# First opening's loads split by use, half 0's forward transform in PSUM banks 4 to 7, three offset adds on VectorE

## What is computed

```python
mod = silu(c) @ w_ada[l] + b_ada[l]                 # the "ada" pieces
u, gate = adaln_modulate(h, mod)                    # the opening
p = split_proj(u @ w_in[l])

def hyena_filter_spectrum(n, ...):                  # in the opening too
    h = sin(fr * (h @ w + b))                       # three times: the "net" steps
    h = (h @ w4).reshape(n, ORDER, 2, W) * exp(-t * deltas)   # the "tap" steps
    return rfft(full)                               # the "blk" steps

def hyena_mix(xv, gate, conv_w, spec, bias):
    x1, x2, v = split(depthwise_conv(xv, conv_w), 3)
    z = x1 * long_conv(v, 0)                        # order 0
    z = x2 * long_conv(z, 1)                        # order 1
    return z * silu(gate)

h = layer_norm(ALPHA * h + gate * out) * ln_g + ln_b    # gained, then the offset
```

## Time and profile before

| | us |
|---|---|
| median of 3 runs (all: 2884.63, 2884.56, 2879.94) | 2884.56 |
| the profiled execution | 2881.1 |
| its span | 2879.3 |
| TensorE busy in it | 2697.6 (94%) |
| VectorE busy | 1601.5 (56%) |
| ACT busy | 1013.9 (35%) |
| GpSimd busy | 590.3 (21%) |

### The profile page before, as it was taken

How to read it: one execution, slowest core, us unless ns; L and a number is a source line. 1 busy time by engine, 2 the same in 40 slices (tenths; PEclk the granted TensorE clock), 3 DMA queues, 4 the chain that set the end, 5 groups by cost and what they waited for, 6 DMA issues and landing times.

```text
span 2879.3 us, 50275 instructions
## 1 busy us (share of the span) xinstructions
PE 2697.6 (94%) x21222; PEld 2152.7 (75%) x21222; DVE 1601.5 (56%) x2789; ACT 1013.9 (35%) x1642; POOL 590.3 (21%) x243
## 2 busy tenths in 40 slices
PE   7899998999999999999999999888899999999997
PEld 1388777887888888887787438677778787887775
DVE  4745777427564443436747654667537754453756
ACT  0335444222222343224432234454333334423533
POOL 0022000120113211321024312100140132232036
PEclk8999999999999999999999999999999999999998
DMA  7321000332222112220134551100143231231034
GB/s 248 137 73 47 16 20 16 110 110 88 75 87 88 66 52 98 86 81 30 39 113 152 196 183 53 37 14 14 54 160 103 100 117 55 97 116 59 25 115 168
DMA packets 94237, 251.71 MB, mean 87 GB/s; under 512 B 10466, under 2 KB 28132, under 8 KB 93632
## 3 DMA queue, kind: packets, MB, share of 16 engines
q1 hardware_dynamic: 83322, 220.84, 22.7%
q10 hardware_dynamic: 10694, 27.67, 2.6%
HBM read 207.05 MB, written 34.08 MB: 84 GB/s over the span
## 4 chain that ended last, share of the span: by engine, by line
PE 74%; DVE 16%; ACT 4%; issue 3%; DMA 2%; ACTq 1%; POOL 0%; SPq 0%; DVEq 0%
PE ps L912 17%; PE ps L913 17%; PE ps L914 17%; PE ps L920 4%; PE ps L1494 4%; PE ps L1051 2%; PE ps L1521 2%; PE ps L929 2%; DVE t_gcv L2175 1%; PE ps L1504 1%; PE ps L1006 1%; PE ps L1518 1%; PE ps L1097 1%; PE ps L1366 1%; DVE t_grp L2509 1%
## 5 line engine op out<-in xcount | busy, mean ns | idle before, releaser
L873 POOL TENSOR_TENSOR t_wlo<-t_raw,t_whi 128x1024 fp32r<-128x1024 f32 x230 | 568.5, 2473 | 2258.2 <-ACT t_whi L1615 2258.2
L912 PE MATMUL ps<-t_u_hi,t_whi 128*128 128x512 f32 (+1 forms) x2368 | 859.0, 363 | 17.5 <-issue 3.7
L913 PE MATMUL ps<-t_u_lo,t_whi 128*128 128x512 f32 (+1 forms) x2368 | 835.1, 353 | 0.0
L914 PE MATMUL ps<-t_u_hi,t_wlo 128*128 128x512 f32 (+1 forms) x2368 | 830.8, 351 | 0.0
L1615 ACT ACTIVATE t_whi<-t_raw 128x1024 fp32r<-128x1024 f32 x248 | 262.1, 1057 | 843.0 <-PE ps L914 765.8
L912 PEld LDWEIGHTS ps<-t_u_hi,t_whi 128*128 128x128 f32 x2368 | 450.0, 190 | 91.7 <-issue 24.1
L914 PEld LDWEIGHTS ps<-t_u_hi,t_wlo 128*128 128x128 f32 x2368 | 448.3, 189 | 63.6
L913 PEld LDWEIGHTS ps<-t_u_lo,t_whi 128*128 128x128 f32 x2368 | 450.3, 190 | 56.7 <-issue 1.7
L1686 ACT ACTIVATE t_grp<-ps 128x512 f32<-128x512 f32 (+2 forms) x236 | 104.1, 466 | 228.8 <-PE ps L929 107.7
L2778 DVE TENSOR_REDUCE t_amx<-ps 128x1 f32<-128x768 f32 (+1 forms) x120 | 101.5, 846 | 148.8 <-PE ps L1494 148.1
L2167 DVE TENSOR_TENSOR t_yv<-t_oT,t_sil 128x768 f32<-128x768 f32 (+1 forms) x32 | 67.4, 2107 | 174.6 <-ACT t_sil L1686 174.6
(11 more groups left out here) (282 smaller groups left out, 3870.3 us busy)
## 6 DMA issues: line engine op xcount, KB each, us to landing
t_raw<-in_w_in SPq DMA_DIRECT2D x184, 512.0 KB, 3.5
t_raw<-in_w_ada SPq DMA_DIRECT2D x48, 512.0 KB, 4.4
t_raw<-in_w_br SPq DMA_DIRECT2D x32, 512.0 KB, 3.6
t_raw<-in_w_out SPq DMA_DIRECT2D x32, 512.0 KB, 3.7
t_sg<-gate_logits SPq DMA_DIRECT2D x28, 384.0 KB, 4.5
hs<-t_hstage ACTq DMA_DIRECT2D x20, 512.0 KB, 3.7
t_hring<-hs SPq DMA_DIRECT2D x20, 512.0 KB, 5.4
t_prob<-t_pT ACTq DMA_DIRECT2D x56, 128.0 KB, 2.1
```

The lines of the kernel that those rows point to most:

```text
L873: pool.tensor_tensor(wlo[:, c % CONV, :], raw[:, s % RAW, :], whi[:, c % CONV, :].bitcast(f32), ALU.subtract).then_inc(sems["w_ready"], 1)
L912: pe.matmul(o, lh, rh, start=first, stop=False)
L913: pe.matmul(o, lh, rl, start=False, stop=False)
L914: return pe.matmul(o, ll, rh, start=False, stop=last)
```

## The change

- Step "w4" of layer 0's opening goes ahead of ada group 1.
- ACT's loads of layer 0: w4 and bias behind net 0; the four context decays behind net 1, on ld_par; the constants behind net 2, ahead of the latent decays, the residual tiles and the masks; the masks count on ld_h. The waits' numbers follow.
- In both layers and both orders, the forward transform of half 0 of the latents goes to banks 6, 7 (odd) and 4, 5 (even); the transposes of tiles 2 and 3 go to slots 0 and 1, each to the slot of the projection that it reads. TensorE's wait for `hinv` goes from ahead of the forward transform to ahead of the inverse; ACT's copy goes from behind tile 3's conv step to behind the second copy into z, one projection earlier.
- In layer 1, VectorE makes the offset adds of tiles 0 to 2 right behind `gained`, instead of GpSimd.

```diff
         yield "turn", 0, 0
+        yield "w4", 0, 0
         for q in range(4):
             yield "ada", 1, q
-        yield "w4", 0, 0
...
+        def forward_at(st, m):
+
+            return 0 if st or m else 4
...
-                if s + 1 == len(STREAM) or STREAM[s + 1][0] != l:
-                    for i in range(NT if l == 0 else LT - 1):
-                        pool.wait_ge(sems["wo_g"], (NT if l else 0) + i + 1)
+                if l == 0 and STREAM[s + 1][0] != l:
+                    for i in range(NT):
+                        pool.wait_ge(sems["wo_g"], i + 1)
...
                         if st and a == 0:
-                            pe.wait_ge(sems["ld_c"], 112)
+                            pe.wait_ge(sems["ld_c"], 96)
...
                     for lo, name, reader in ((2, "f_fo", "hy_oc"), (0, "f_ev", "hy_ps")):
-                        claim(lo, lo + 1)
+                        at = forward_at(0, m) + lo
+                        claim(at, at + 1)
...
                     if o == 0:
-                        freed["hy_oc"] = freed.get("hy_oc", 0) + 1
-                        pe.wait_ge(sems["hy_oc"], freed["hy_oc"])
+                        pe.wait_ge(sems["ld_ftab"], 16 * (23 if l else 14))
+                        freed["hy_oc"] = turned = freed.get("hy_oc", 0) + 1
...
-                            to_tok(o, m, freed["cv_done"] + m - 3, m)
+                            to_tok(o, m, freed["cv_done"] + m - 3, (nslot[0] + m) % 2)
...
+                            if o == 0:
+                                pe.wait_ge(sems["hy_oc"], turned)
                             ln.take("hy_y")
...
+                        if a == 1 and l == 0:
+                            for dst, src in context_decays():
+                                act.dma_start(dst, src).then_inc(sems["ld_par"], 16)
+                        if a == 2 and l == 0:
                             act.dma_start(cst[:, 1:8, :], A["cst"][:, 1:8, :]).then_inc(sems["ld_c"], 16)
-                        if a == 2 and l == 0:
...
-                            act.dma_start(mask_f[:, :], A["masks"]).then_inc(sems["ld_c"], 16)
+                            act.dma_start(mask_f[:, :], A["masks"]).then_inc(sems["ld_h"], 16)
...
-                    if o == 0:
-                        act.wait_ge(sems["ld_ftab"], 16 * (23 if l else 14))
-                        ln.done(run(hinv[:, :, :, :], y[:, 1, 0:2 * LAT].rearrange("p (e s r) -> p e r s", e=2, r=CLASS),
-                                    ACT.Copy), "hy_oc")
+                        if j == 2 and o == 0:
+                            act.wait_ge(sems["ld_ftab"], 16 * (23 if l else 14))
+                            ln.done(run(hinv[:, :, :, :],
+                                        y[:, 1, 0:2 * LAT].rearrange("p (e s r) -> p e r s", e=2, r=CLASS), ACT.Copy),
+                                    "hy_oc")
...
-            def gained(i):
+            def gained(l, i):
 
                 ln.take("wo_x")
                 x = acc_t[:, i, :]
                 ln.done(tt(x, x, lng[:, 0, :], ALU.mult), "wo_g")
+                if l and i < LT - 1:
+                    ln.own("wo_g")
+                    ln.done(tt(x, x, lng[:, 1, :], ALU.add), "wo_out")
...
+                    if l == 0 and x == 0 and t == 0:
+                        dve.wait_ge(sems["ld_par"], 112)
                     if l == 0 and x == 2 and t == 0:
-                        dve.wait_ge(sems["ld_h"], 16 * (NT + 16))
+                        dve.wait_ge(sems["ld_h"], 16 * (NT + 17))
```

More of the change, by code:

```diff
@@ L544, in latent_decays, with context_decays @@
                     yield dec[32 * k:32 * k + 32, r, :], A["dec"][r:P:CLASS, k, :]
+        def context_decays():
+            for r in range(CT):
+                for half in range(2):
+                    yield dec[64 * half:64 * half + 64, LT + r, :], A["dec"][r:P:2, LT + half, :]
         def filter_inputs(l):
@@ L551, in filter_inputs @@
                 yield from latent_decays()
-            for r in range(CT):
-                for half in range(2):
-                    yield dec[64 * half:64 * half + 64, LT + r, :], A["dec"][r:P:2, LT + half, :]
+                yield from context_decays()
         def residual(l, i):
@@ L1362, in forward @@
                     for lo, name, reader in ((2, "f_fo", "hy_oc"), (0, "f_ev", "hy_ps")):
-                        claim(lo, lo + 1)
+                        at = forward_at(0, m) + lo
+                        claim(at, at + 1)
                         for r in range(lo, lo + 2):
                             for e in range(2):
-                                last = pe.matmul(ps[:, r, e * 256:e * 256 + 256], htab[:, r, e, :],
+                                last = pe.matmul(ps[:, at + r - lo, e * 256:e * 256 + 256], htab[:, r, e, :],
                                                  z[:, r, m * 256:m * 256 + 256], start=True, stop=True)
                         ln.done(last, name)
-                        lend(reader, lo, lo + 1)
+                        lend(reader, at, at + 1)
                 def inverse(m, i):
@@ L1991, in hyena @@
                             odd[0] += 1
-                            ln.done(run(h_odd[:, :, :], ps[:, 2:4, :], ACT.Copy), "hy_oc")
+                            x = forward_at(st, m) + 2
+                            ln.done(run(h_odd[:, :, :], ps[:, x:x + 2, :], ACT.Copy), "hy_oc")
                         elif st:
@@ L2292, in open_layer @@
                     if kind == "masks":
-                        dve.wait_ge(sems["ld_c"], 112)
+                        dve.wait_ge(sems["ld_c"], 96)
+                        dve.wait_ge(sems["ld_h"], 16 * (NT + 17))
                         full = mask_f[:, :].rearrange("p (a b c) -> p a b c", a=2, b=LEVELS)
@@ L2325, in open_layer @@
                     if kind == "gain":
-                        gained(a)
+                        gained(l - 1, a)
                     if kind == "stat":
@@ L2631, in apart @@
                         dve.wait_ge(sems["hy_iv"], i - 1)
-                    tt(two[:, 0, :, :], ps[:, 0:2, :], h_odd[:, :, :], ALU.add)
-                    ln.step(tt(two[:, 1, :, :], ps[:, 0:2, :], h_odd[:, :, :], ALU.subtract), "hy_ps")
+                    tt(two[:, 0, :, :], ps[:, x:x + 2, :], h_odd[:, :, :], ALU.add)
+                    ln.step(tt(two[:, 1, :, :], ps[:, x:x + 2, :], h_odd[:, :, :], ALU.subtract), "hy_ps")
                     dve.wait_ge(sems["hy_tr"], turned)
@@ L2853, in project_out @@
                     if kind == "gain":
-                        gained(a)
+                        gained(l, a)
             for l in range(DEPTH):
```

20 lines of the change are left out of this document (10 added, 10 removed).

## The result

| | before | after |
|---|---|---|
| median, us (runs) | 2882.25 (2879.29 to 2884.63, 4) | 2858.81 (2855.68 to 2868.26, 4) |
| profiled execution, us (span) | 2881.1 (2879.3) | 2861.72 (2859.9) |

The ratio is 0.9926 (95%: 0.9902 to 0.995): 23.4 us faster between the medians, 19.4 between the two profiled spans. The forecast was 2851, with 31.5 us of gain; the measured time is inside its range, and it is also the figure of rival A, 2859.

What follows compares the result with a forecast made beforehand. TensorE, busy 94% of the span, was taken as the bound. Opening 12.5 plus Hyena 20.0 minus tail 1.0 gave 31.5 us, so 2849.6 from the profiled 2881.1, predicted as 2851 us; range 2837 to 2866.

Steps and rivals of the forecast that it cites:

- rival A: Opening: loads move no sooner, masks still land near 67 us, opening gains 5 to 8 us; 2859 us, chance 0.12.
- Group 1's piece, 5.3 us: Opening, TensorE: without 1 MB of loads beside its w_ada piece, group 1 ends near 26.0 instead of 31.3 us.
- w4's sum moved, first tap 5.0 us earlier: Opening: VectorE sums w4 before group 1's row, so TensorE's first tap starts at 36.9 instead of 41.91 us.
- Masks' wait on TensorE, 5.7 and 1.45 us: First context transform: the 5.71 us wait on the masks' counter goes, and its 8 matmuls run 1.45 us faster.
- Masks' landing at 60.7: Opening: masks land at 60.7 instead of 67.0 us; VectorE's first latent tap wants them at 59.7.
- The slow clock of 40 to 50 us, 3.3 us: Opening, two taps and the w_ada group between: a shorter TensorE wait may keep the clock up, 0 to 3.3 us.
- rival C: Other stops of about 1.3 us at new times pull the clock down two or three times; 2860 us, chance 0.08.
- Opening, sum 12.5: Gain up to the latent taps: 13.9 us with the clock held, 12.1 with it lost, taken as 12.5.
- Hyena, 20.0: Hyena stage, upper banks and earlier hinv copy: 7.4 and 3.6 us in layer 0, 7.4 and 1.6 in layer 1.
- Rival B: VectorE sets the pace in the Hyena stage, only its shifts count, 16.3 us; 2855 us, chance 0.12.
- Tail, -1.0: End of layer 1: offset adds on VectorE instead of GpSimd make the tail 1.0 us slower, bounds -0.9 and +2.
- D and E: D: early loads delay w_ada pieces, 2889 us, 0.04. E: forward still waits in ACT's order, 2874 us, 0.04.

Runs made afterwards that it cites:

- opening part alone: Only the opening's edits (w4's sum ahead of group 1's row, loads by use, masks on ld_h) against the kernel before: 2876.96 us, ratio 0.9972.
- loads alone: Kernel before with only the new order of ACT's loads and their semaphores, w4's sum not moved: 2872.79 us, ratio 0.9963.
- the late version: Changed kernel with masks issued behind the first spectrum's stores on their own semaphore, VectorE's tap waiting for decays alone: 2855.53, again 2852.64 us.
- the one with a semaphore of its own: Changed kernel with masks issued where the change issues them but counted on a separate semaphore, VectorE's tap waiting for decays only: 2862.66 us, ratio 0.9934.
- hinv copy alone: Kernel before with only the hinv copy made earlier and TensorE's wait for it ahead of the inverse, banks as before: 2881.7 us, ratio 0.9985.
- the copy's place: Kernel before with the Hyena edits, but the hinv copy at its old place in ACT's order: 2869.35 us, ratio 0.9945.

## Why the prediction was right, and where it wasn't

**Sign and range: right. Size: 8 us too much gain**, from two steps of the opening and, in the profiled pair, from the rest of the kernel. That the median meets rival A's 2859 is partly luck: A had 5 to 8 us in the opening (4.7 in the pair, 7.7 over more traces), and nothing lost in the rest.

- **Group 1's piece, 5.3 us: nearly right.** It ends 4.5 us earlier (26.8 for 31.3) and runs at full clock, but TensorE still waits 0.91 us for the piece, and 0.88 to 2.31 in the other traces with the new loads.
- **w4's sum moved, first tap 5.0 us earlier: failed.** It came 1.2 us earlier in the pair; over the six traces with the old opening the tap stands at 41.2 us on average (39.9 to 42.5), over the six with the sum moved and the new loads at 39.0 (38.0 to 40.7). The step took it that TensorE's group 2 would run unhindered from 28.6 on. Its own pieces are late by 2.20, 1.44 (the changed kernel again), 0.62 (opening part alone) and 1.04 us (loads alone), and once a stop was followed by the low clock (7.01 us for 12 matmuls, 5.31 elsewhere). TensorE's total wait for pieces went from 5.4 to 5.0 us: part of the stop moved on to the next group. The kernel with the loads alone has its tap at 38.42 us and its opening at 136.5, within the spread of those with the move.
- **Masks' wait on TensorE, 5.7 and 1.45 us: right.** Transform without wait and at 3.70 us. In the five other traces with the old opening this wait was 3.6 to 8.6 us.
- **Masks' landing at 60.7: failed.** That was rival A, and its mechanism is what the rows show: the load is issued 8.5 us earlier and takes 7.6 us longer. The engines had 9.5 MB to move between the start of ACT's queue and the landing instead of 7.9, and were full from 50 to 66 us before and after. The forecast moved the landing with the issue. Where they land, 64.5 to 66.2 us in the four traces that show it, VectorE's tap waits 1.53, 3.97, 3.85 and 5.57 us. Without a wait (the late version and the one with a semaphore of its own) it stands at 61.15 us, in the second late trace at 60.38. The Trainium skill (DMA: Bandwidth & Descriptors, Queues, rings and completion order) says each DMA engine takes turns between its queues. The traces show both queues moving at once, but not the half of the rate that I drew from it for SP's pieces: from 55 to 60 us ACT's queue moved 1.50 MB and SP's 0.39 (before: 1.47 and 0.57), and one piece on SP's queue needed 16.61 us beside ACT's loads. I gave this case 0.12, and weighed it by the DMA share of 0.77 from 40 to 50 us; from 50 to 66, where the masks travel, it was 1.00 already, and I hadn't read that stretch.
- **The slow clock of 40 to 50 us, 3.3 us: open, and not all the change's to win.** At the first tap it was gone in all traces with the new loads (1.99 us, 3.04 in the first trace before), but also in three of six with the old opening, the kernel before again among them. Falls came at 30 to 38 and, in some executions, behind the 1.2 to 1.8 us stops at 74 and 88 us: the mechanism of rival C, at one or two places.
- **Opening, sum 12.5:** 4.7 in the profiled pair. Over the traces it took 144.2 us in six executions with the old opening (standard deviation 2.1), 136.5 in three with the new (2.1), and 129.2 in two with the masks late: 7.7 and 15.0 us.
- **Hyena, 20.0:** 19.9 in the pair. Every new wait is within 0.3 us of its term. Rival B is out by layer 0, which wins 11.6 us where VectorE's shifts alone gave 7.8; layer 1's 8.3 don't separate the two (B 8.5, forecast 9.0). Over seven traces each (the old ones with the hinv copy alone among them) the two stretches take 410.0 and 390.8 us: 19.2.
- **Tail, -1.0: one term missed, 0.0.** After, the last evacuation starts 13.5 us before the end, before 15.6, so its path is 2.1 us shorter and it starts 2.1 us later behind the last matmul, nearly as forecast (1.9). The sum then lacked one term. Before, VectorE's product behind it (the first row) ran beside GpSimd's two adds (the second):

```profile
2864.50 1.64 DVE L2175 SCALAR_TENSOR_TENSOR t_acc<-t_oT,t_acc 128x512 f32<-128x512 f32 x1
```

```profile
2860.43 5.17 POOL L879 TENSOR_TENSOR t_acc<-t_acc,t_lng 128x1024 f32<-128x1024 f32 x2
```

After, it takes 0.69:

```profile
2847.17 0.69 DVE L2191 SCALAR_TENSOR_TENSOR t_acc<-t_oT,t_acc 128x512 f32<-128x512 f32 x1
...
2851.96 4.87 DVE L2183 TENSOR_TENSOR t_acc<-t_acc,t_lng 128x1024 f32<-128x1024 f32 x4
```

  -1.9 + 2.1 - 1.2 + 0.95 comes to 0.0. I had counted what GpSimd's third add took from VectorE, but not its first two. By the same rule of the Trainium skill (SBUF — State Buffer, section SBUF: two separate sides) that I cited for the others, this one was to be expected. The rows fit: GpSimd's adds are over at 2865.6 and the product, which takes 0.69 us alone, at 2866.1. No run tests it apart.
- **The rest, 0: open.** The pair loses 5.1 us where nothing was edited. Over all traces this rest took 2306.9 us (standard deviation 7.6) in the seven kernels with the old Hyena stage and 2313.9 (4.3) in the seven with the new; its low-clock time was 92 and 103 us. That is 7 us with a standard error near 3.3 (7.6 and 4.3, each over the root of 7, combined): it would close the sum (7.7 + 19.2 - 7 = 20 against medians 23.4 and 18.3 apart), but other scatter of the clock does as well, and no run separates a lasting give-back from it.
- **D and E** had nothing for them: one piece did take 16.61 us, and cost TensorE 2.25; another took 18.01 (loads alone) and cost 3.68.

## What to carry to other kernels

An earlier issue was an earlier landing here only as far as the DMA engines had room in between: before moving a landing time with its issue, add up the bytes that must pass up to the landing, read the DMA share there, and ask which transfers a less idle engine will now start. The better edit was to take the load that is wanted last out of the full stretch and give it a semaphore of its own. And where two waits stand one behind the other, as those for the hinv copy and for the banks did, lifting one shows the other (3.89 us became 3.00): test the edits singly before keeping both. Here that was done for the hinv edit and for the copy's place; the banks with TensorE's wait for hinv at its old place were not run.

## What the runs showed of the hardware

- The same kernel, with TensorE's idle time equal to 0.3 us, had its granted clock low for 129.7 us up to the last matmul in one execution and 119.5 in another, at different places: the stretch from matmul 13161 to 17519 had 33.4 and 10.5 us of it. Two traces are no ground for a few microseconds in a stretch that nobody edited.
- The 896 KB of masks took 20.70 us from issue to landing in the changed kernel, from 45.5 us on, and 13.05 in the kernel before, from 54.0 on; the DMA share was 1.05 and 1.00 from 50 to 66 us. With the masks issued at the same place (own semaphore, share 1.04), a 512 KB piece took 16.61 us; the median of its kind was 4.4 over the kernel before.
- Two queues at work on full DMA engines did not get equal parts: 1.50 MB on ACT's and 0.39 MB on SP's from 55 to 60 us (worked out from the packets of the changed kernel's trace).
- VectorE's product of two SBUF operands, 128x512, took 0.69 us alone and 1.64 beside a GpSimd add.
